# Two-layer hybrid decoder trunk: the router reads the rows before they are normed, and the norm scale moves into the experts' silu, product and softmax

## The chip, the cores and the metric

The kernel runs on one core of one Trainium2 chip. The metric is the device time of one execution in microseconds (us). TensorE is called PE here, VectorE DVE, ScalarE ACT, GpSimd POOL and the queue that issues most transfers SP.

## What is computed

The trunk has two layers over 256 tokens of width 1024. The change lies in the last part of the second layer: after the residual sum `h` is complete, the rows are normed, a router picks two of eight experts for each token, and the experts' SwiGLU outputs are added with softmax weights.

```python
def rms_norm(x, g):
    y = x * rsqrt(mean(x * x, axis=-1) + EPS)
    return y * g

def moe_swiglu(xn, w_router, we_gate, we_up, we_down):    # xn = rms_norm(h, ln_ffn1)
    logits = xn @ w_router                                # 256 x 8
    top_v, top_i = top_k(logits, 2)
    top_w = softmax(top_v)
    gates = sum(one_hot(top_i, 8) * top_w[..., None], axis=-2)
    y = 0
    for e in range(8):                                    # D_FF = 3584
        y = y + gates[:, e:e+1] * ((silu(xn @ we_gate[e]) * (xn @ we_up[e])) @ we_down[e])
    return y                                              # h + y is the output
```

The norm's scale is one number for each token. It doesn't change the order of a token's logits, and a product of a row with a matrix can be scaled after as well as before.

## The kernel before, in words

Each engine runs a program that is written out by hand in one order; semaphores tie the programs together, so an instruction that waits holds up everything behind it on its engine. Tokens lie in two blocks of 128 (`TB = 2`). Products of full precision are made of split operands: ACT writes the high part of a weight piece (`w_hi`, `split_high`, L1091), DVE the low part (`w_lo`, `split_low`, L1555), and PE does three matmuls for each (`TERMS`, L465). A piece is 128 x 1024; six pieces (`SPLIT_SLOTS`) and six chunks of two pieces (`RAW_SLOTS`) are held at a time, and SP fetches a chunk when DVE has split the one in its slot.

After the last projection of the attention part, `h` is final, and the router stage begins. PE transposes the 16 blocks of `h` (L477). ACT sums the squares of the rows (`sumsq`, L1100) and writes the turned rows' high parts (`xT_hi`, L1127), DVE computes the norm's scale by a chain of small steps (`rsqrt`, L1571 to L1577) and writes the low parts (`xT_lo`, L1597) and the normed rows `xr` (L2067). PE forms turned logits (`wr_hi`, `wr_lo`), DVE copies them, PE turns them back (L921). DVE ranks the logits of both token blocks, works out which token uses which expert (`rt`), the softmax weights through ACT's exponential (L1438), the positions (`posc`, from PE's products of masks with `before` and `ones`), the table of all units (`tab`), and marks the tokens of unit 0 in `onehot` (L2120). Then it works out tables for up to three extra units (`over`, L2127 to L2140), which are needed only if an expert has more than 128 tokens.

A unit is one expert with up to 128 of its tokens. For unit 0 PE gathers the rows by products of `xr` with `onehot` (`gather`) and turns the slots' gate and token number (`turn`, `cur`); ACT and DVE split the gathered rows (`gathered`, L1447 and L2148). A later unit's rows come by an indirect transfer from `x_rows`, which POOL has written from `xr`. A unit has seven steps over D_FF; the gate products go to one bank, ACT takes their silu (`silu_g`, L1457), the up products to another, DVE multiplies them (`act_f`, L2188), PE turns the product (L986), ACT and DVE split it (L1461, L2192), and PE multiplies by the down weights. ACT keeps a unit's gate in `gslot` (`keep_gate`, L1467). `keep_busy(n, 6)` (L485) is n transposes into a bank that nobody reads.

Of the kernel before, what the change touches and what calls it, by code (L numbers as in the profile page):

```python
# [12 lines left out]
P = 128  # L13
# [19 lines left out]
def hybrid_trunk(  # L33
# [37 lines left out]
    with ExitStack() as ctx:  # L71
# [27 lines left out]
        earlier = sb("earlier", [P, NE, NE])  # L99
        gain_rows = sb("gain_rows", [P, P])  # L100
# [9 lines left out]
        wr_hi = sb("wr_hi", [P, KD, NE], F32R)  # L110
        wr_lo = sb("wr_lo", [P, KD, NE], F32R)
# [50 lines left out]
        with part:  # L162
# [8 lines left out]
            lgT = sb("lgT", [NE, S], scope=part)  # L171
            lg = sb("lg", [P, TB, NE], scope=part)
            rt = sb("rt", [P, 16, TB, NE], scope=part)
            cmp = sb("cmp", [P, 3, TB, NE, NE], scope=part)
            posc = sb("posc", [P, TB + 1, NE], scope=part)
            tab = sb("tab", [P, UNITS, 3, TB], scope=part)
            cur = sb("cur", [P, 4, TB], scope=part)
            over = sb("over", [P, 8, NE], scope=part)
            unit_f = sb("unit_f", [1, 4], scope=part)
            unit_i = sb("unit_i", [1, 4], I32, scope=part)  # L180
            gslot = sb("gslot", [P, 1], scope=part)
            xg = sb("xg", [P, D], scope=part)
            y_out = sb("y_out", [P, D], scope=part)
            slot = sb("slot", [P, 2], scope=part)
# [208 lines left out]
        def _(pool):  # L393
# [28 lines left out]
            fill(earlier[:, :, :], 1.0, [[1, NE], [-1, NE]], -1, 0, ALU.is_ge, 0.0)  # L422
            fill(headsel[:, :, :], 0.0, [[-1, LH], [0, P]], 0, 1, ALU.not_equal, 1.0)
# [10 lines left out]
            pool.wait_ge(sem("rows_normed"), 8)  # L434
            pool.dma_start(tokens(x_rows), xr[:, :, :]).then_inc(sem("x_rows_here"), 16)
# [27 lines left out]
        def _(pe):  # L463
# [444 lines left out]
            transpose_rows(lambda t, k: h[:, t, k * P:(k + 1) * P], KD, after=("rows_added", 2 * TB))  # L908
            wr = (wr_hi, wr_lo)
            keep_busy(24, 6)  # L910
            for k in range(KD):
                if k % 2 == 0:
                    pe.wait_ge(sem("xT_ready"), 26 + k // 2 + 1)
                for a, b in TERMS:
                    last = mm(B[4][0:NE, 0:S], wr[a][:, k, :], xT[b][:, k, :],
                              k == 0 and (a, b) == (0, 0), k == KD - 1 and (a, b) == TERMS[-1])
            last.then_inc(sem("logits_psum"), 1)

            pe.wait_ge(sem("logits_copied"), 1)
            for t in range(TB):  # L920
                last = pe.transpose(B[5][:, S + t * NE:S + (t + 1) * NE], lgT[:, t * P:(t + 1) * P], ident[0:NE, 0:NE])  # L921
            last.then_inc(sem("logits_psum"), 1)

            keep_busy(10, 6)
            pe.wait_ge(sem("routed"), 1)
# [8 lines left out]
            def gather(u):  # L934

                pe.wait_ge(sem("onehot_ready"), u + 1)
                for k in range(KD):
                    for t in range(TB):
                        last = mm(B[k // 4][:, (k % 4) * P:(k % 4 + 1) * P], xr[:, t, k * P:(k + 1) * P],
                                  F(onehot[:, t, :]), t == 0, t == TB - 1)  # L940
# [73 lines left out]
            def start_unit(u):  # L1014

                gather(u)
                turn(u)
                pe.wait_ge(sem("gather_ready"), 2 * u + 2)
                e_in(C_MOE, 0, FFN_CHUNKS * u)

# [41 lines left out]
            for j in range(NU_MAX):  # L1062
                n_over = pe.value_load(unit_i[0:1, 3:4], min_val=0, max_val=NU_MAX)
                with pe.If(n_over > j):
                    start_unit(NE + j)
# [4 lines left out]
        def _(act):  # L1070
# [364 lines left out]
            norm_rows(("tile_evacuated", (copied(TILE_OUT1),) * TB))  # L1435
            high_T(KD, 26, G["ffn1"])
            act.wait_ge(sem("top_diff"), 1)
            act.activation(rt[:, 8, :, 0:1], rt[:, 7, :, 0:1], ACT.Exp).then_inc(sem("top_exp"), 1)  # L1438
            act.activation(small[:, 63:64], iota[:, 0:1], ACT.Silu)
# [11 lines left out]
            def e_silu(c, more, n):  # L1451
# [5 lines left out]
                act.activation(silu_g[:, 0:FC], B[0][:, :], ACT.Silu).then_inc(sem("esilu_done"), 1)  # L1457
# [6 lines left out]
            def keep_gate(u):  # L1464

                act.wait_ge(sem("slots_known"), u + 1)
                act.activation(gslot[:, :], slot[:, 0:1], ACT.Copy).then_inc(sem("turned"), 1)  # L1467

            def unit(u, last=False):
# [43 lines left out]
                if not last:  # L1513
                    act.wait_ge(sem("y_scaled"), 2 * u + 2)
                    keep_gate(u + 1)

            gathered(0)
            keep_gate(0)
# [4 lines left out]
            for j in range(NU_MAX):  # L1523
                n_over = act.value_load(unit_i[0:1, 3:4], min_val=0, max_val=NU_MAX)
                with act.If(n_over > j):
# [4 lines left out]
                    keep_gate(NE + j)  # L1530
# [4 lines left out]
        def _(dve):  # L1535
# [275 lines left out]
            chain(dve.tensor_copy(wr_hi[:, :, :], w_router[:, :, :]))  # L1811
            dve.tensor_tensor(wr_lo[:, :, :], w_router[:, :, :], F(wr_hi[:, :, :]), ALU.subtract).then_inc(
# [243 lines left out]
            add_tile(TILE_OUT1 + 1, C_OUT1 + 2, 1)  # L2056

# [7 lines left out]
            low_T(KD, 26, G["ffn1"])  # L2065
            for t in range(TB):
                dve.tensor_scalar(xr[:, t, :], h[:, t, :], stat[:, 4, 36 + t:37 + t], None, ALU.mult).then_inc(  # L2067
                    sem("rows_normed"), 1)
            dve.wait_ge(sem("logits_psum"), 1)
# [219 lines left out]
```

## Time and profile before

| | |
|---|---|
| median of 3 runs | 1539.64 us (1538.36 to 1540.07) |
| the profiled execution's own time | 1541.83 us |
| its span in the profile | 1540.1 us |
| PE busy | 1476.1 us, 96% of the span |
| DVE busy | 1210.4 us, 79% |
| ACT busy | 1049.4 us, 68% |
| POOL busy | 39.3 us, 3% |
| last matmul of the projection before the router starts | 528.74 us after the span's start |
| first matmul of unit 0's experts | 553.96 us |

Busy shares are means over stages with different limits. The router stage, from about 529 to 554 us, is read by itself: there PE has little of its own to do and its program holds 68 matmuls of `keep_busy`.

### The profile page before, as it was taken

What the parts mean: (1) busy time and instruction counts of PE and PEld (TensorE: products, weight loads), DVE (VectorE), ACT (ScalarE), POOL (GpSimd) and SP (SyncE); (2) the same over time, 40 slices, a digit from 0 to 9 for tenths busy, and PEclk for the clock granted to TensorE, in tenths of its full rate; (3) what the DMA queues carried; (4) which work ended last, traced back from release to release, by engine and by line L of the source; (5) the groups of instructions that cost most, each with busy time, mean ns of one, the idle gap of its engine ahead of it and who ended that gap; (6) DMA issues with size and microseconds to landing.
All of it is one profiled execution on the core that took longest, in us unless ns stands there. A gap on an engine that the chain in (4) does not pass through costs nothing.

```text
span 1540.1 us, 23433 instructions
## 1 busy us (share of the span) xinstructions
PE 1476.1 (96%) x7724; PEld 1258.2 (82%) x7724; DVE 1210.4 (79%) x1571; ACT 1049.4 (68%) x1381; POOL 39.3 (3%) x83
## 2 busy tenths in 40 slices
PE   6998999999998899999999999999999999999995
PEld 5987999999786778878878888888888888887884
DVE  6967555445566589989989989989989998998993
ACT  5664544444485457788777878878778878787872
POOL 1000000000000000000010000000000000000000
PEclk9999999999999999999999999999999999999997
DMA  7554365555251369999999999999999999999990
GB/s 256 175 178 137 103 227 184 177 184 180 70 178 55 110 230 388 375 356 378 390 348 380 390 357 375 390 370 357 393 377 343 393 380 351 390 379 355 396 391 33
DMA packets 191804, 442.05 MB, mean 287 GB/s; under 512 B 8750, under 2 KB 20364, under 8 KB 191756
## 3 DMA queue, kind: packets, MB, share of 16 engines
q1 hardware_dynamic: 188636, 429.90, 77.1%
q0 software_dynamic: 3120, 11.54, 2.7%
q8 instruction: 28, 0.46, 0.1%
q14 instruction: 20, 0.16, 0.0%
HBM read 433.54 MB, written 7.86 MB: 287 GB/s over the span
## 4 chain that ended last, share of the span: by engine, by line
PE 90%; DVE 6%; ACT 3%; issue 1%; DMA 0%; ACTq 0%; SPq 0%; DVEq 0%
PE bank L465 87%; PE bank L986 2%; DVE w_lo L1555 1%; ACT w_hi L1091 1%; DVE xT_lo L1597 1%; PE bank L477 0%; ACT xT_hi L1127 0%; DVE aT_lo L2192 0%; PE bank L485 0%; ACT aT_hi L1461 0%; DMA late<-in_mem_dram 0%; PE bank L653 0%; ACT scr L1409 0%; DVE stat L1575 0%; DVE stat L1576 0%
## 5 line engine op out<-in xcount | busy, mean ns | idle before, releaser
L1555 DVE TENSOR_TENSOR w_lo<-raw,w_hi 128x1024 fp32r<-128x1024 f32 (+1 forms) x832 | 959.3, 1196 | 202.7 <-ACT w_hi L1091 190.7
L1091 ACT ACTIVATE w_hi<-raw 128x1024 fp32r<-128x1024 f32 (+1 forms) x832 | 841.2, 1043 | 246.4 <-PE bank L465 239.6
L465 PE MATMUL bank<-w_hi,xT_hi 128*128 128x512 f32 (+4 forms) x1118 | 436.0, 390 | 11.9 <-DVE w_lo L1555 3.6
L465 PE MATMUL bank<-w_hi,xT_lo 128*128 128x512 f32 (+4 forms) x1118 | 429.0, 384 | 0.0
L465 PE MATMUL bank<-w_lo,xT_hi 128*128 128x512 f32 (+4 forms) x1118 | 428.4, 383 | 0.0
L465 PEld LDWEIGHTS bank<-w_hi,xT_hi 128*128 128x128 f32 x1118 | 211.0, 189 | 54.4 <-issue 6.6
L465 PEld LDWEIGHTS bank<-w_hi,xT_lo 128*128 128x128 f32 x1118 | 210.9, 189 | 40.3
L465 PEld LDWEIGHTS bank<-w_lo,xT_hi 128*128 128x128 f32 x1118 | 211.2, 189 | 37.2
L465 PE MATMUL bank<-w_hi,aT_hi 128*128 128x512 f32 x560 | 220.1, 393 | 7.3 <-DVE aT_lo L2192 5.7
L465 PE MATMUL bank<-w_lo,aT_hi 128*128 128x512 f32 x560 | 220.3, 393 | 0.0
L465 PE MATMUL bank<-w_hi,aT_lo 128*128 128x512 f32 x560 | 218.2, 390 | 0.0
L465 PE MATMUL bank<-xT_hi,w_hi 128*128 128x256 f32 x544 | 155.2, 285 | 2.4 <-DVE w_lo L1555 1.7
L465 PE MATMUL bank<-xT_hi,w_lo 128*128 128x256 f32 x544 | 154.7, 284 | 0.0
L465 PE MATMUL bank<-xT_lo,w_hi 128*128 128x256 f32 x544 | 154.7, 284 | 0.0
L465 PEld LDWEIGHTS bank<-w_hi,aT_hi 128*128 128x128 f32 x560 | 105.1, 188 | 33.0 <-issue 7.9
L465 PEld LDWEIGHTS bank<-w_hi,aT_lo 128*128 128x128 f32 x560 | 105.1, 188 | 23.2
L465 PEld LDWEIGHTS bank<-w_lo,aT_hi 128*128 128x128 f32 x560 | 105.3, 188 | 21.1
L465 PEld LDWEIGHTS bank<-xT_hi,w_hi 128*128 128x128 f32 x544 | 103.9, 191 | 3.4 <-DVE w_lo L1555 2.0
L465 PEld LDWEIGHTS bank<-xT_lo,w_hi 128*128 128x128 f32 x544 | 103.9, 191 | 0.2
L465 PEld LDWEIGHTS bank<-xT_hi,w_lo 128*128 128x128 f32 x544 | 103.8, 191 | 0.0
L1461 ACT ACTIVATE aT_hi<-bank 128x512 fp32r<-128x512 f32 x56 | 33.5, 598 | 52.0 <-PE bank L986 51.9
L2192 DVE TENSOR_TENSOR aT_lo<-bank,aT_hi 128x512 fp32r<-128x512 f32 x56 | 38.6, 689 | 14.4 <-ACT aT_hi L1461 10.7
(345 smaller groups left out, 790.5 us busy)
## 6 DMA issues: line engine op xcount, KB each, us to landing
raw<-in_we_gate_dram SPq DMA_DIRECT2D x112, 1024.0 KB, 7.8
raw<-in_we_up_dram SPq DMA_DIRECT2D x112, 1024.0 KB, 8.0
raw<-in_we_down_dram SPq DMA_DIRECT2D x112, 1024.0 KB, 7.2
raw<-in_w_gate_dram SPq DMA_DIRECT2D x14, 1024.0 KB, 5.1
raw<-in_w_up_dram SPq DMA_DIRECT2D x14, 1024.0 KB, 5.1
raw<-in_w_down_dram SPq DMA_DIRECT2D x14, 1024.0 KB, 4.8
raw<-in_w_in_dram SPq DMA_DIRECT2D x16, 768.0 KB, 4.9
raw<-in_w_out_dram SPq DMA_DIRECT2D x8, 1024.0 KB, 5.0
```

Source lines behind the costliest of these rows:

```text
L465: return pe.matmul(o, a, b, start=start, stop=stop, skip_group_check=True, **kw)
L986: last = pe.transpose(B[2][:, q * P:(q + 1) * P], act_f[:, q * P:(q + 1) * P], ident[:, :])
L1091: act.activation(split_piece(w_hi, c, shape, half), raw_piece(c, shape, half), ACT.Copy).then_inc(hi_ready, 1)
L1461: act.activation(aT_hi[:, :, 0:P], B[2][:, :].rearrange("p (q s) -> p q s", q=FB), ACT.Copy).then_inc(sem("eaT_hi"), 1)
L1555: dve.tensor_tensor(split_piece(w_lo, c, shape, half), raw_piece(c, shape, half), F(split_piece(w_hi, c, shape, half)), ALU.subtract).then ...
L1597: ins = dve.scalar_tensor_tensor(out=xT_lo[:, k0 + k, :], in0=B[bank0 + b][:, kk * S:(kk + 1) * S], scalar=1.0 if gain is None else gains[ ...
L2192: dve.tensor_tensor(aT_lo[:, :, 0:P], B[2][:, :].rearrange("p (q s) -> p q s", q=FB), F(aT_hi[:, :, 0:P]), ALU.subtract).then_inc(sem("eaT ...
```

## The change

- PE transposes `h` into four banks; ACT and DVE copy them as plain fp32 into `act_f` and `silu_g`, which are free then. The router's logits are fp32 matmuls of these with `wr_gain`, the router weights times the norm's weights, which DVE has made long before. They come out with tokens in partitions, unscaled by the norm.
- DVE ranks each token block when its logits are there (`route`), and marks unit 0's tokens in `onehot` directly from `posc`. The chain for the norm's scale, the logits' difference and the exponential come after that.
- Unit 0 is gathered from `h` itself; `x_rows` is written from `h`; ACT copies `h` to `xr` for extra units. So the expert products lack the norm's scale: `turn` brings it along in `cur` (three columns in place of two), `gslot` holds gate and scale, silu takes `scale=gslot[:, 1:2]`, the product becomes a `scalar_tensor_tensor` with the scale, and the difference of logits is multiplied by it before the exponential.
- `gate_weights` (softmax weights and unit table) stands behind `gathered(0)` on DVE, `turn(0)` behind the first gate product on PE, `keep_gate(u)` ahead of the first silu of each unit on ACT, and `extra_units` between units 6 and 7 on DVE.
- `keep_busy` has 20 and 6 matmuls in place of 24, 10, 12 and 22.

```diff
@@ pool
-            pool.wait_ge(sem("rows_normed"), 8)
-            pool.dma_start(tokens(x_rows), xr[:, :, :]).then_inc(sem("x_rows_here"), 16)
+            pool.wait_ge(sem("rows_added"), 3 * TB)
+            pool.dma_start(tokens(x_rows), h[:, :, :]).then_inc(sem("x_rows_here"), 16)
@@ tensor
-            transpose_rows(lambda t, k: h[:, t, k * P:(k + 1) * P], KD, after=("rows_added", 2 * TB))
-            keep_busy(24, 6)
...
-            keep_busy(10, 6)
-            pe.wait_ge(sem("routed"), 1)
+            hT = (act_f, silu_g)
+            for t in range(TB):
+                pe.wait_ge(sem("rows_added"), 2 * TB + t + 1)
+                for k in range(KD):
+                    last = pe.transpose(B[2 * t + k // 4][:, (k % 4) * P:(k % 4 + 1) * P], h[:, t, k * P:(k + 1) * P], ident[:, :])
+                    if k % 4 == 3:
+                        last.then_inc(sem("router_psum"), 1)
+            for t in range(TB):
+                pe.wait_ge(sem("router_first"), t + 1)
+                pe.wait_ge(sem("router_second"), t + 1)
+                for k in range(KD):
+                    last = mm(B[4 + t][:, 0:NE], hT[t][:, k * P:(k + 1) * P], wr_gain[:, k, :], k == 0, k == KD - 1)
+                last.then_inc(sem("logits_psum"), 1)
+
+            keep_busy(20, 6)
+            pe.wait_ge(sem("routed"), TB)
...
             def turn(u):
+                pe.wait_ge(sem("cur_ready"), u + 1)
                 for t in range(TB):
-                    last = mm(B[3][:, S:S + 2], F(onehot[:, t, :]), cur[:, 2:4, t], t == 0, t == TB - 1)
+                    last = mm(B[3][:, S:S + 3], F(onehot[:, t, :]), cur[:, 2:5, t], t == 0, t == TB - 1)
...
-            keep_busy(12, 6)
-            gather(0)
-            turn(0)
-            keep_busy(22, 6)
-            pe.wait_ge(sem("gather_ready"), 2)
-            e_in(C_MOE, 0, 0)
+            keep_busy(6, 6)
+            start_unit(0, first=True)
@@ scalar
+            act.wait_ge(sem("tile_evacuated"), copied(TILE_OUT1))
+            for t in range(TB):
+                sumsq(h[:, t, 0:512], 2 * t, xr[:, t, 0:512]).then_inc(sem("sumsq_ready"), 1)
+            for t in range(TB):
+                act.wait_ge(sem("router_psum"), 2 * t + 1)
+                act.activation((act_f, silu_g)[t][:, 0:512], B[2 * t][:, :], ACT.Copy).then_inc(sem("router_first"), 1)
...
-                act.activation(silu_g[:, 0:FC], B[0][:, :], ACT.Silu).then_inc(sem("esilu_done"), 1)
+                act.activation(silu_g[:, 0:FC], B[0][:, :], ACT.Silu, scale=gslot[:, 1:2]).then_inc(sem("esilu_done"), 1)
...
                 for j in (4, 5):
                     split_high(p0 + j, UP, more, lap)
+                keep_gate(u)
+                act.wait_ge(sem("turned"), u + 1)
                 e_silu(C_MOE + 2, more, None)
@@ vector
+            for t in range(TB):
+                dve.wait_ge(sem("router_psum"), 2 * t + 2)
+                dve.tensor_copy((act_f, silu_g)[t][:, 512:1024], B[2 * t + 1][:, :]).then_inc(sem("router_second"), 1)
+            def route(t):
+                dve.wait_ge(sem("logits_psum"), t + 1)
+                chain(dve.tensor_copy(lg[:, t, :], B[4 + t][:, 0:NE]))
...
+                step(dve.tensor_tensor(equal, other, own, ALU.is_equal))
+                step(dve.tensor_tensor(above, other, own, ALU.is_gt))
+                settle()
+                chain(dve.tensor_tensor(equal, equal, earlier[:, :, :], ALU.mult))
+                chain(dve.tensor_reduce(rt[:, 0, t, :], cmp[:, t], AX, ALU.add))
+                dve.tensor_scalar(rt[:, 5, t, :], rt[:, 0, t, :], 1.5, None, ALU.is_lt).then_inc(sem("routed"), 1)
...
-                dve.tensor_tensor(act_f[:, 0:FC], B[1][:, :], silu_g[:, 0:FC], ALU.mult).then_inc(sem("eact_done"), 1)
+                dve.scalar_tensor_tensor(out=act_f[:, 0:FC], in0=B[1][:, :], scalar=gslot[:, 1:2], in1=silu_g[:, 0:FC],
+                                         op0=ALU.mult, op1=ALU.mult).then_inc(sem("eact_done"), 1)
...
             gathered(0)
+            gate_weights()
+            split_low(2 * C_MOE + 4, UP)
             slots(0)
-            for j in (4, 5):
-                split_low(2 * C_MOE + j, UP)
+            split_low(2 * C_MOE + 5, UP)
             with dve.Fori(0, NE - 1) as u:
                 unit(u)
+            extra_units()
             unit(NE - 1, last=True)
```

`gate_weights` and `extra_units` hold what stood in DVE's program ahead of `gathered(0)`: the first the softmax weights, `tab` and `cur`, the second the tables of the extra units, now for all three at once (18 instructions).

PE's program between the logits and the first expert product, before (`before` and `ones` are constant masks, `ident` alone is `keep_busy`, `onehot,xr` the gather, `cur,onehot` the turn, and the last row is the first expert matmul):

```order
L921 MATMUL bank<-ident,lgT 128x8 [waits logits_copied]
L921 MATMUL bank<-ident,lgT 128x8
L485 MATMUL bank<-ident 128x128 x10
L465 MATMUL bank<-rt,before 128x8 [waits routed]
L465 MATMUL bank<-rt,ones 128x8
L465 MATMUL bank<-rt,before 128x8
L465 MATMUL bank<-rt,ones 128x8 x2
L485 MATMUL bank<-ident 128x128 x12
L465 MATMUL bank<-onehot,xr 128x128 [waits onehot_ready]
L465 MATMUL bank<-cur,onehot 128x2 x2
L485 MATMUL bank<-ident 128x128 x22
L465 MATMUL bank<-w_hi,xT_hi 128x512 [waits lo_ready,gather_ready]
```

The same place after the change:

```order
L468 MATMUL bank<-wr_gain,silu_g 128x8 x7
L488 MATMUL bank<-ident 128x128 x20
L468 MATMUL bank<-rt,before 128x8 [waits routed]
L468 MATMUL bank<-rt,ones 128x8
L468 MATMUL bank<-rt,before 128x8
L468 MATMUL bank<-rt,ones 128x8 x2
L488 MATMUL bank<-ident 128x128 x6
L468 MATMUL bank<-onehot,h 128x128 [waits onehot_ready]
L468 MATMUL bank<-onehot,h 128x128 x15
L468 MATMUL bank<-w_hi,xT_hi 128x512 [waits lo_ready,gather_ready]
...
L468 MATMUL bank<-cur,onehot 128x3 [waits cur_ready]
L468 MATMUL bank<-cur,onehot 128x3
```

The 22 transposes between gather and first product are gone, and the turn has moved behind the 24 matmuls that begin with the row on `gather_ready`.

DVE's program from the end of the gathered rows' low parts into unit 0, before (the first row is the last wait of `gathered(0)`, then `slots(0)` and pieces 4 and 5):

```order
L2148 SCALAR_TENSOR_TENSOR xT_lo<-bank,gains,xT_hi 128x128 [waits gather_hi]
L2148 SCALAR_TENSOR_TENSOR xT_lo<-bank,gains,xT_hi 128x128 x3
L2157 COPY slot<-bank 128x2 [waits turn_psum]
L2160 TENSOR_SCALAR no_token<-slot,row_no 128x1 [waits slot_copied]
L2163 SCALAR_TENSOR_TENSOR rows_next<-slot,no_token 128x1 [waits no_token_ready]
L1555 TENSOR_TENSOR w_lo<-raw,w_hi 128x1024 [waits hi_ready] x2
```

And after the change:

```order
L2169 SCALAR_TENSOR_TENSOR xT_lo<-bank,gains,xT_hi 128x128 [waits gather_hi]
L2169 SCALAR_TENSOR_TENSOR xT_lo<-bank,gains,xT_hi 128x128 x3
L2115 TENSOR_SCALAR rt<-rt 128x2 [waits top_exp]
...
L2126 COPY tab<-rt 128x2x8 x2
L2132 COPY cur<-tab 128x6 [waits dve_step]
L1563 TENSOR_TENSOR w_lo<-raw,w_hi 128x1024 [waits hi_ready]
L2178 COPY slot<-bank 128x3 [waits turn_psum]
L2181 TENSOR_SCALAR no_token<-slot,row_no 128x1 [waits slot_copied]
L2184 SCALAR_TENSOR_TENSOR rows_next<-slot,no_token 128x1 [waits no_token_ready]
L1563 TENSOR_TENSOR w_lo<-raw,w_hi 128x1024 [waits hi_ready]
```

The gate's chain now stands behind the gathered rows, and piece 5 waits on DVE behind the turn.

## Rows read from the trace of the kernel before

**Rows 1.** The page's chain that ended last, by engine.

```profile
PE 90%; DVE 6%; ACT 3%; issue 1%; DMA 0%; ACTq 0%; SPq 0%; DVEq 0%
```

**Rows 2.** Who PE waited for from 554 to 1540 us: total, times, longest.

```profile
PE bank L465 <- DVE aT_lo L2192: 5.7, 8, 1.4
PE bank L465 <- DVE w_lo L1555: 1.4, 8, 0.2
```

**Rows 3.** Timeline of DVE, router stage: start, us, instruction, idle time and its releaser.

```profile
529.17 0.69 DVE L1834 TENSOR_TENSOR h<-bank,h 128x512 f32<-128x512 f32 x1 [2.03 <-PE bank L465]
530.65 0.16 DVE L2061 TENSOR_REDUCE stat<-stat 128x2 f32<-128x4 f32 x1 [0.79 <-ACT xr L1100]
...
533.66 3.23 DVE L1597 SCALAR_TENSOR_TENSOR xT_lo<-bank,gains,xT_hi 128x256 fp32r<-128x256 f32 x8 [0.28 <-ACT xT_hi L1127]
...
538.91 0.36 DVE L2073 TENSOR_SCALAR lg<-bank,stat 128x8 f32<-128x8 f32 x2 [0.38 <-PE bank L921]
...
544.34 0.17 DVE L2117 COPY cur<-tab 128x6 f32<-128x6 f32 x1
544.55 0.60 DVE L2120 TENSOR_SCALAR onehot<-iota,cur 128x128 fp32r<-128x128 f32 x2
...
551.77 2.14 DVE L2148 SCALAR_TENSOR_TENSOR xT_lo<-bank,gains,xT_hi 128x128 fp32r<-128x128 f32 x8
553.84 0.14 DVE L2157 COPY slot<-bank 128x2 f32<-128x2 f32 x1
```

**Rows 4.** Timeline of PE in the same stage.

```profile
528.97 2.04 PE L477 MATMUL bank<-ident,h 128*128 128x128 f32 x16
...
541.69 0.39 PE L465 MATMUL bank<-rt,before 128*128 128x8 f32 x2 [1.58 <-DVE rt L2093]
...
543.10 2.80 PE L485 MATMUL bank<-ident 128*128 128x128 f32 x12
545.69 3.88 PE L465 MATMUL bank<-onehot,xr 128*128 128x128 f32 x32
549.40 0.51 PE L465 MATMUL bank<-cur,onehot 128*128 128x2 f32 x4
549.77 2.60 PE L485 MATMUL bank<-ident 128*128 128x128 f32 x22
553.96 0.50 PE L465 MATMUL bank<-w_hi,xT_hi 128*128 128x512 f32 x1 [1.60 <-DVE xT_lo L2148]
```

**Rows 5.** Timeline of ACT, gather and start of unit 0.

```profile
549.60 1.14 ACT L1447 ACTIVATE xT_hi<-bank,gains 128x128 fp32r<-128x128 f32 x4 [0.64 <-PE bank L465]
...
559.77 0.60 ACT L1457 ACTIVATE silu_g<-bank 128x512 f32<-128x512 f32 x1 [3.05 <-PE bank L465]
```

**Rows 6.** Groups of the whole span by form: busy us, mean ns.

```profile
L1461 ACT ACTIVATE aT_hi<-bank 128x512 fp32r<-128x512 f32 x56 | 33.5, 598 | 52.0 <-PE bank L986 51.9
L1511 ACT ACTIVATE y_out<-bank,gslot 128x512 f32<-128x512 f32 x14 | 8.9, 685 | 6.4 <-PE bank L465 6.4
L2188 DVE TENSOR_TENSOR act_f<-bank,silu_g 128x512 f32<-128x512 f32 x56 | 38.5, 688 | 0.0
L2171 DVE SCALAR_TENSOR_TENSOR ys_lo<-bank,gslot,ys_hi 128x512 fp32r<-128x512 f32 x2 | 1.4, 747 | 6.7 <-ACT ys_hi L1511 6.7
```

**Rows 7.** Windows: busy time (x count) of PE, PEld, DVE, ACT, POOL; PE clock; DMA.

```profile
540.00:541.00 1.00, 0.11 (x2) 0.00 (x0) 0.91 (x4) 0.00 (x0) 1.00 (x2) 1.00 1.03 414
543.00:544.00 1.00, 1.00 (x7) 1.00 (x7) 0.93 (x8) 0.71 (x2) 0.00 (x0) 0.50 1.02 393
553.00:554.00 1.00, 0.04 (x1) 0.04 (x1) 0.97 (x5) 0.00 (x0) 0.00 (x0) 1.00 0.00 0
620.00:640.00 20.00, 20.00 (x94) 16.55 (x93) 18.32 (x17) 15.62 (x18) 0.00 (x0) 1.00 1.03 383
```

**Rows 8.** Timeline at the start of unit 7.

```profile
1406.73 4.63 DVE L1555 TENSOR_TENSOR w_lo<-raw,w_hi 128x1024 fp32r<-128x1024 f32 x4 [1.91 <-ACT w_hi L1091]
1408.01 0.50 PE L465 MATMUL bank<-w_hi,xT_hi 128*128 128x512 f32 x1 [0.18 <-DVE w_lo L1555]
```

More of the change, by code:

```diff
@@ L422, in _ @@
             fill(earlier[:, :, :], 1.0, [[1, NE], [-1, NE]], -1, 0, ALU.is_ge, 0.0)
+            for j in range(NU_MAX):
+                step(pool.memset(nth[:, j, :], float(j + 1)))
             fill(headsel[:, :, :], 0.0, [[-1, LH], [0, P]], 0, 1, ALU.not_equal, 1.0)
@@ L1466, in keep_gate @@
                 act.wait_ge(sem("slots_known"), u + 1)
-                act.activation(gslot[:, :], slot[:, 0:1], ACT.Copy).then_inc(sem("turned"), 1)
+                act.activation(gslot[:, :], slot[:, 0:2], ACT.Copy).then_inc(sem("turned"), 1)
             def unit(u, last=False):
@@ L1514, in unit @@
                     act.wait_ge(sem("y_scaled"), 2 * u + 2)
-                    keep_gate(u + 1)
             gathered(0)
-            keep_gate(0)
+            act.wait_ge(sem("top_diff"), 1)
+            act.activation(rt[:, 8, :, 0:1], rt[:, 7, :, 0:1], ACT.Exp).then_inc(sem("top_exp"), 1)
+            act.activation(small[:, 63:64], iota[:, 0:1], ACT.Silu)
             with act.Fori(0, NE - 1) as u:
@@ L2075, in _ @@
-            settle()
-            for t in range(TB):
-                own = lg[:, t, :].unsqueeze(2).to_broadcast([P, NE, NE])
-                other = lg[:, t, :].unsqueeze(1).to_broadcast([P, NE, NE])
-                step(dve.tensor_tensor(cmp[:, 0, t], other, own, ALU.is_gt))
-                step(dve.tensor_tensor(cmp[:, 1, t], other, own, ALU.is_equal))
-            settle()
-            for t in range(TB):
-                step(dve.tensor_tensor(cmp[:, 1, t], cmp[:, 1, t], earlier[:, :, :], ALU.mult))
@@ L2101, in _ @@
-            chain(dve.tensor_tensor(rt[:, 10, :, 0:1], rt[:, 8, :, 0:1], rt[:, 9, :, 0:1], ALU.mult))
-            for t in range(TB):
-                step(dve.tensor_scalar(rt[:, 11, t, :], rt[:, 1, t, :], rt[:, 9, t, 0:1], None, ALU.mult))
-            settle()
-            for t in range(TB):
-                step(dve.scalar_tensor_tensor(out=rt[:, 12, t, :], in0=rt[:, 2, t, :], scalar=rt[:, 10, t, 0:1],
-                                              in1=rt[:, 11, t, :], op0=ALU.mult, op1=ALU.add))
@@ L2108, in _ @@
-            dve.wait_ge(sem("slots_psum"), 1)
-            chain(dve.tensor_copy(posc[:, :, :].rearrange("p t e -> p (t e)"), B[5][:, 0:3 * NE]))
-            for n, src in enumerate((posc[:, 0:TB, :], rt[:, 5], rt[:, 12])):
-                step(dve.tensor_copy(tab[:, 0:NE, n, :].rearrange("p e t -> p t e"), src))
-            chain(dve.tensor_copy(cur[:, 3, :], row_no[:, 0:TB]))
+            scale = stat[:, 4, 36:36 + TB]
+            step(dve.tensor_copy(cur[:, 3, :], scale))
+            step(dve.tensor_copy(cur[:, 4, :], row_no[:, 0:TB]))
@@ new lines, in _, with gate_weights @@
+            chain(dve.tensor_tensor(rt[:, 6], rt[:, 4], rt[:, 3], ALU.subtract))
+            chain(dve.tensor_reduce(rt[:, 7, :, 1], rt[:, 6], AX, ALU.add))
+            dve.tensor_tensor(rt[:, 7, :, 0], rt[:, 7, :, 1], scale, ALU.mult).then_inc(sem("top_diff"), 1)
+            def gate_weights():
+                dve.wait_ge(sem("top_exp"), 1)
+                chain(dve.tensor_scalar(rt[:, 9, :, 0:1], rt[:, 8, :, 0:1], 1.0, None, ALU.add))
+                chain(dve.reciprocal(rt[:, 9, :, 0:1], rt[:, 9, :, 0:1]))
+                chain(dve.tensor_tensor(rt[:, 10, :, 0:1], rt[:, 8, :, 0:1], rt[:, 9, :, 0:1], ALU.mult))
+                for t in range(TB):
+                    step(dve.tensor_scalar(rt[:, 11, t, :], rt[:, 1, t, :], rt[:, 9, t, 0:1], None, ALU.mult))
+                settle()
+                for t in range(TB):
+                    step(dve.scalar_tensor_tensor(out=rt[:, 12, t, :], in0=rt[:, 2, t, :], scalar=rt[:, 10, t, 0:1],
+                                                  in1=rt[:, 11, t, :], op0=ALU.mult, op1=ALU.add))
+                settle()
+                for n, src in enumerate((posc[:, 0:TB, :], rt[:, 5], rt[:, 12])):
+                    step(dve.tensor_copy(tab[:, 0:NE, n, :].rearrange("p e t -> p t e"), src))
+                settle()
+                current(0)
```

135 lines of the change are left out of this document (61 added, 74 removed).

## The prediction

> **What bounds the kernel now.** I read the page's chain that ended last first: 90% of the span is PE's own work [rows 1]. Then the waits of PE in the expert stage, 554 to 1540 us: the longest sum is 5.7 us, once per unit for the last product's low part, and 1.4 us are eight waits of 0.2 us for a weight piece at a unit's start [rows 2]. So that stage is as long as its matmuls, and nothing in it gets shorter. What is left is the stage between, and the timelines show it: PE transposes `h` from 528.97 and begins the first expert matmul at 553.96 [rows 4], 25.0 us later. Its last wait there is for DVE, whose timeline has nearly no gap [rows 3]: the norm's chain 530.65 to 533.4, the turned rows' low parts to 536.9, `xr`, ranking from 538.91, softmax and tables, `onehot` ready at 545.15, then 6.6 us of tables for extra units, and only at 551.77 the gathered rows' low parts, though ACT had their second half ready at 550.74 [rows 5]. The change takes most of these off DVE's path.
>
> **The router up to the marks.** The 16 transposes end at 531.0 as before; the first eight at about 530.0. DVE copies half of block 0 out of its bank: no such row here is shown, the nearest is the sum of the same size out of a bank, 0.69 us [rows 3]. So logits of block 0 can start at 530.8, when PE's own transposes are through. They are 8 fp32 matmuls with 8 columns. Masks of the same shape took 1.41 us for 5 (541.69 to 543.10), 0.28 each, partly at the lower clock; the gather 3.88 us for 16, 0.24 [rows 4]. I take 0.23: block 0 to 532.7, block 1 to 534.5; by 0.28 it would be 0.8 us more. Ranking both blocks took 2.7 us (538.91 to PE's masks at 541.69); now block 0's lies under PE's logits of block 1, and half, 1.4 us, is left: 535.95. PE meanwhile has 20 transposes of `keep_busy`. 22 took 2.60 us, the last one's latency included, so 0.11 each and 2.2 us for 20, to 536.7: PE comes 0.7 us after the masks are ready to go. Masks 1.4 us (538.1), copy of `posc` 0.2, marks 0.60 [rows 3]: `onehot` is ready at about 538.9 against 545.15.
>
> **Gather and first product.** The gather takes 3.9 us as before, to 542.7. ACT needs 1.14 us for the second half [rows 5], 543.85, DVE half of 2.14 us [rows 3], 544.95, and the first expert matmul starts at 545.05 in place of 553.96: **8.9 us gained**. DVE must do the norm's chain in this time: 2.75 us (530.65 to 533.4) and some 1.1 us for `cur`, difference and product, so 538.9 to 542.75. It comes to the first half of the gathered rows 0.7 us after ACT, is through at 543.8, and so just in time for the second. Here the cover is about 0.05 us; every further delay of that chain counts in full. The exponential, the table load and the gate's chain lie behind, under the 5.8 us of the first product (553.96 to 559.77 [rows 4, 5]).
>
> **Start of unit 0.** The turn is now between the first product and the up product: 0.5 us on PE [rows 4]. Piece 5's low part waits on DVE behind the slots, which wait for the turn: turn done at 551.35, three small instructions to 551.9 (0.14 us for the first [rows 3], with its latencies about 0.2 each), piece 5 at 1.16 us (4.63 for 4 [rows 8]) to 553.1, while PE is through with piece 4 at 552.65: 0.45 us of waiting. ACT copies `gslot` and takes the silu, both behind the slots, 0.8 us, then piece 6 at about 1.05 and DVE's 1.16: 555.0, where PE wants it at 554.45: 0.6 us. Before, there was a wait of 0.2 [rows 2] and no turn. **Loss 1.35 us.** The SP fetches that piece 5 frees also come this much nearer to PE, but six chunks are held.
>
> **Steady stage.** Silu gets a scale from memory. The same read out of a bank took 598 ns without and 685 with such a scale [rows 6]: 0.09 us. DVE's product goes from 688 to about the 747 of the same form with a scalar from memory [rows 6]: 0.06 us, 56 times. DVE is busy 18.32 of 20 us in a window of this stage [rows 7], so 1.4 us of each step of 16.9 are free and this is hidden; without that cover it would be 3.4 us. The silu is hidden too, but for unit starts, where piece 6 stands behind it and PE waits 0.18 us for that piece [rows 8]: 6 times 0.09, **loss 0.5 us**. The Trainium skill, page ScalarE: Activation LUTs, section What ACT_TABLE_LOAD costs, gives about 93 ns for each pointer operand of an ACTIVATE; the rows give 87, and the loss would come to 0.56 us by the page. The extra units' tables now stand at one unit's start. They are 18 small instructions, partly overlapped; before, such steps came every 0.2 us, and I take 2.7 us. DVE is idle 1.91 us there [rows 8], so **0.8 us are lost**, between nothing and 1.7 (0.2 us each without overlap). `keep_gate` moves from one idle place of ACT to another: nothing. Three memsets of POOL at the start and one small instruction less on DVE: nothing, under the first transfers and under PE's work.
>
> **Sum without the clock:** 8.9 - 1.35 - 0.5 - 0.8 = 6.25 us.
>
> **The clock.** In the window 543 to 544 the granted clock is 0.50, that is 1.2 GHz [rows 7], and 12 transposes took 2.80 us there, where 22 took 2.60 at 2.4 GHz [rows 4]. Ahead of it lay 1.58 us of idle PE and masks of 8 columns. Another idle time of 1.60 us, before 553.96, was followed by nothing of the kind: 1.00 [rows 7]. The changed program has more of what came before the fall: 3.7 us of matmuls with 8 columns, and an idle PE of about 2.3 us (542.7 to 545.05) with no transposes in it, where 22 lay before. The low stretch of before lasted some 3 us and cost little, since DVE was late anyway. Now PE's work stands on the path nearly everywhere, and such a stretch costs half its length, 1.6 us. [...] I count one such stretch: gain 4.65 us. The profiled execution took 1541.83 us and would take 1537.2; the median of the runs lies 2.2 us lower, and the forecast for it is 1539.64 - 4.65 = **1535.0 us**.
>
> **The rivals.**
> - *No fall of the clock* (chance 0.28): 1533.4 us. For it: the gap at 553 was not followed by one.
> - *Forecast, one stretch at 1.2 GHz* (0.41): 1535.0; its own range is 1534 to 1536.5.
> - *Two or three stretches, or a router priced at the upper bounds* (0.22): if transposes run at 1.2 GHz ahead of the masks, 20 of them take 4.6 us and the marks come 2.4 us later, and the first product loses another 1.6 us: gain about 2, 1537.6; with 0.8 us more for the logits 1538.4. This is within 0.2% of before.
> - *Slower: PE at 1.2 GHz for the whole stage* (0.06). Logits, transposes, masks, gather, turn and first product are some 17 us of PE's work at 2.4 GHz; all of it at half speed adds over 12 us and gives about 1546. It decides from 9.3 us of loss on (6.25 plus 3.1). Against it: the fall in before gave way again under transposes and gather, at 549.77 transposes came every 0.11 us [rows 4].
> - *DVE becomes the bound of the steady stage* (0.03): the product would have to take 1.4 us more, not 0.06, before the first is felt, and 1.55 more to end 0.2% slower; the row of 747 ns speaks against it. A transfer as the bound belongs here: the DMA share is 1.03 in 620 to 640 [rows 7]. If the weights set the pace, the gain would be that of the next fetch, which hangs on piece 5's low part: near 5 us, and the losses at unit starts would vanish. That too lands at 1535.
>
> **Range and chances.** The low end is the case without a fall, with the extra tables hidden and a little cheaper logits: 1532.4. The high end is the case of three stretches: 1538.9. A measurement of this kernel tells about 0.2%, 3.1 us, from no change. Faster than 1536.6: no fall, most of one stretch: 0.70. Within: 0.23. Slower: 0.07.
>
> **What would show it.** In the profile of the changed kernel: `onehot` marks end near 539 and the first expert matmul is near 545, 16 us after the transposes' start; PE's wait ahead of it is for DVE's `xT_lo`; the logits' matmuls lie 0.23 us apart; PE waits about 0.5 us each for pieces 5 and 6 of unit 0; unit 7 begins with a wait near 1 us for `w_lo`; silu is at 0.68, the product at 0.75, and no other wait is new between units. The expert stage is 1.5 to 3 us longer from its first matmul to its end. The prediction is wrong if the clock stays low for long, if DVE's chain for the norm's scale ends late and pushes the gathered rows, or if the product or silu bring new waits in each of the 56 steps.

## The result, and the profile after

The changed kernel takes 1546.07 us (median of 14 runs, 1541.73 to 1548.45), the kernel before 1540.96 beside it (1538.36 to 1543.04): ratio 1.0031, 95% interval 1.0023 to 1.0039. It is slower by 5.1 us, where 4.65 us of gain were forecast. The profiled execution took 1544.55 us, with a span of 1542.8.

Yet the router stage went nearly as the prediction said. PE's timeline in the profile after, with the rows that answer to [rows 4]:

```profile
531.09 2.04 PE L915 MATMUL bank<-ident,h 128*128 128x128 f32 x16
533.00 1.92 PE L468 MATMUL bank<-wr_gain,act_f 128*128 128x8 f32 x16
534.78 1.93 PE L468 MATMUL bank<-wr_gain,silu_g 128*128 128x8 f32 x16
536.57 4.05 PE L488 MATMUL bank<-ident 128*128 128x128 f32 x20
540.45 0.29 PE L468 MATMUL bank<-rt,before 128*128 128x8 f32 x2
...
541.48 0.85 PE L488 MATMUL bank<-ident 128*128 128x128 f32 x6
542.64 3.84 PE L468 MATMUL bank<-onehot,h 128*128 128x128 f32 x32 [0.30 <-DVE onehot L2092]
548.87 0.50 PE L468 MATMUL bank<-w_hi,xT_hi 128*128 128x512 f32 x1 [2.39 <-DVE xT_lo L2169]
...
554.49 0.51 PE L468 MATMUL bank<-cur,onehot 128*128 128x3 f32 x4
...
556.83 0.50 PE L468 MATMUL bank<-w_hi,xT_hi 128*128 128x512 f32 x1 [0.35 <-DVE w_lo L1563]
...
558.93 0.50 PE L468 MATMUL bank<-w_hi,xT_hi 128*128 128x512 f32 x1 [0.44 <-DVE w_lo L1563]
```

From the transposes of `h` to the first expert matmul it is 17.78 us, where it was 24.99: 7.2 us less. The 20 transposes of `keep_busy` took 4.05 us. The windows say why (busy time of PE, PEld, DVE, ACT, POOL, then PE's clock and the DMA share):

```profile
537.00:540.00 3.00, 3.00 (x16) 3.00 (x15) 1.15 (x7) 0.00 (x0) 0.00 (x0) 0.50 1.01 388
545.00:546.00 1.00, 1.00 (x12) 1.00 (x11) 0.83 (x7) 0.87 (x4) 0.00 (x0) 1.00 0.00 0
```

They ran at 1.2 GHz, half the clock, and DVE, done with ranking at 538.25, then sat idle for the masks:

```profile
538.08 0.17 DVE L2086 TENSOR_SCALAR rt<-rt 128x16 f32<-128x16 f32 x1
541.76 0.18 DVE L2090 COPY posc<-bank 128x24 f32<-128x24 f32 x1 [3.51 <-PE bank L468]
...
546.07 1.12 DVE L2169 SCALAR_TENSOR_TENSOR xT_lo<-bank,gains,xT_hi 128x128 fp32r<-128x128 f32 x4
547.69 1.13 DVE L2169 SCALAR_TENSOR_TENSOR xT_lo<-bank,gains,xT_hi 128x128 fp32r<-128x128 f32 x4 [0.50 <-ACT xT_hi L1453]
```

The time was lost elsewhere. The transposes of `h` begin 2.1 us later than in [rows 4], though little of the code ahead of them is changed. And in the expert stage the sums of PE's waits grew by less than was forecast. From 545 us on, total, times and longest:

```profile
PE bank L468 <- DVE aT_lo L2214: 5.8, 8, 1.4
PE bank L468 <- DVE w_lo L1563: 3.1, 9, 0.7
PE bank L468 <- DVE xT_lo L2169: 2.4, 1, 2.4
```

That is 1.7 us more for `w_lo` than in [rows 2], where 2.15 had been forecast (0.85 in unit 0, 0.5, and 0.8 at unit 7). But from the turn of `act_f` in unit 0's first step to that of the last step of unit 7 it is 947.3 us, after 941.4: 5.9 more. A middle step shows no wait in either kernel and takes 16.96 us in place of 16.87, every time. Both turns of one such step and the first, second and last of its 24 down products, before:

```profile
950.52 0.60 PE L986 MATMUL bank<-ident,act_f 128*128 128x128 f32 x4
...
956.45 0.39 PE L465 MATMUL bank<-w_hi,aT_hi 128*128 128x512 f32 x1
956.68 0.39 PE L465 MATMUL bank<-w_lo,aT_hi 128*128 128x512 f32 x1
...
961.72 0.39 PE L465 MATMUL bank<-w_hi,aT_lo 128*128 128x512 f32 x1
...
967.39 0.27 PE L986 MATMUL bank<-ident,act_f 128*128 128x128 f32 x1
```

And after:

```profile
949.14 0.60 PE L988 MATMUL bank<-ident,act_f 128*128 128x128 f32 x4
...
955.05 0.39 PE L468 MATMUL bank<-w_hi,aT_hi 128*128 128x512 f32 x1
955.29 0.39 PE L468 MATMUL bank<-w_lo,aT_hi 128*128 128x512 f32 x1
...
960.42 0.40 PE L468 MATMUL bank<-w_hi,aT_lo 128*128 128x512 f32 x1
...
966.10 0.27 PE L988 MATMUL bank<-ident,act_f 128*128 128x128 f32 x1
```

The 23 distances between 24 down products are 5.27 us before and 5.37 after: 229 and 233.5 ns each. The other 48 products of a step, with `xT`, lie some 227 ns apart in both. (Over all products from 600 to 1500 us the means are 229.1 and 233.1 ns with `aT`, 227.7 and 227.5 with `xT`.) The clock was 1.00 in both stretches. So the same matmuls on operands of the same shape take longer, and only those that read `aT`.

`aT` is the stationary operand of these matmuls: PE loads a 128x128 piece of it ahead of each one (PEld), and the 512 columns that then stream past are those of the weights, `w_hi` or `w_lo`. The loads' own time is the same, only the idle time between them grew. One of the three groups of loads, 600 to 1500 us (count, busy, mean ns, idle before), in the kernel before and after:

```profile
L465 PEld LDWEIGHTS bank<-w_lo,aT_hi 128*128 128x128 f32 x416 | 78.2, 188 | 15.5
L468 PEld LDWEIGHTS bank<-w_lo,aT_hi 128*128 128x128 f32 x416 | 78.1, 188 | 18.7
```

Over the three groups the idle time is 56.6 us before and 61.7 after.

What differs is where `aT` lies. The change removes `wr_hi` and `wr_lo` (256 bytes of each partition apiece), adds `wr_gain` (256) and `nth` (96), and all that is declared behind them moves down by 160 bytes: `aT_hi` from byte 165184 to 165024, `aT_lo`, 4096 further, likewise. `w_hi`, `w_lo`, `xT_hi` and `xT_lo` stand ahead of them and didn't move; all four begin 128 bytes beyond a multiple of 1024. The four pieces of `aT_hi` that a step loads lie 1024 bytes apart, so all have the remainder by 1024 of the first.

### The profile page after: what moved, and what is told of

The parts are those of the page before. It is cut to its first block, busy times and chain, and to the rows that moved or that the text cites. A ratio compares the mean times of both kernels' runs of the same rounds, so it can differ in the third digit from the quotient of the medians.

```text
span 1542.8 us, 23338 instructions
## 1 busy us (share of the span) xinstructions
PE 1478.9 (96%) x7688; PEld 1255.2 (81%) x7688; DVE 1204.6 (78%) x1547; ACT 1053.2 (68%) x1377; POOL 42.8 (3%) x86
## 4 chain that ended last, share of the span: by engine, by line
PE 90%; DVE 5%; ACT 3%; issue 1%; DMA 0%; ACTq 0%; SPq 0%; DVEq 0%
PE bank L468 87%; PE bank L988 2%; DVE w_lo L1563 1%; ACT w_hi L1090 1%; DVE xT_lo L1605 0%; PE bank L480 0%; DVE aT_lo L2214 0%; PE bank L488 0%; ACT aT_hi L1467 0%; DMA late<-in_mem_dram 0%; PE bank L656 0%; ACT scr L1408 0%; ACT xT_hi L1126 0%; DVE stat L1583 0%; DVE stat L1582 0%
## 5 line engine op out<-in xcount | busy, mean ns | idle before, releaser
L468 PE MATMUL bank<-w_hi,aT_lo 128*128 128x512 f32 x560 | 221.4, 395 | 0.0
```

Of the source, the lines that this page charges most:

```text
L468: return pe.matmul(o, a, b, start=start, stop=stop, skip_group_check=True, **kw)
```

## The experiments

Each run stands beside runs of the kernel before on the same chip; the kernel before had medians of 1540.3 to 1541.4 in all of them. "Ratio" is the time over that of the kernel before, with its 95% interval; "step" is the distance in us between the turns of `act_f` in the middle steps of units 1 to 6.

**Theories.** L: the address of `aT` sets the distance of the down products, and costs what the expert stage lost. Rivals: the new forms of silu and product slow the step; the clock takes it; the router gains nothing.

### First four: shifts, and the old forms

`a_aligned` is the changed kernel with eight fp32 ahead of `cos`, which brings `aT_hi` to 165056, a multiple of 64. `b_shifted` is the kernel before with the same line (165216), `b_shift_behind` the kernel before with it behind `aT_lo`, so that `silu_g` and all behind move and `aT` doesn't.

```diff
+        pad32 = sb("pad32", [P, 8])
         cos = sb("cos", [P, TB, HALF])
```

> The changed kernel with one unused tile of 32 bytes ahead of cos, so that aT_hi and aT_lo begin at a multiple of 64 bytes again, as in the kernel before; nothing else differs. Theory A (the place of aT in SBUF makes the down products' 24 matmuls of a step some 4 ns slower each): a middle step of a unit goes from 16.96 back to 16.87 us, the expert stage gets 5 to 6 us shorter and layer 0's SwiGLU about 1 us, so 1539.5 us, that is 6 to 7 us under the changed kernel and 1 to 2 under the one before, and the clock decides the rest. Theory B (silu with a scale from memory and the three-operand product slow PE's work): the step stays at 16.96 and the time at 1546.

> The kernel before with the same unused 32 bytes ahead of cos, which shifts aT_hi and aT_lo from a multiple of 64 bytes to 32 beyond one. Theory A: a middle step goes from 16.87 to 16.96 us and the time up by 6 to 7 us, to 1547. Theory B: no change.

> The kernel before with the unused 32 bytes between aT_lo and silu_g: aT stays where it was, and all that is declared behind it in this part (silu_g, act_f, onehot and the router's tiles) is shifted. Theory A, aT alone: no change, step 16.87. Rival A2 (the place of silu_g and act_f, which ACT and DVE write while PE multiplies, is what counts): step 16.96 and 6 us more.

`a_old_forms` is the changed kernel with the experts' silu and product in their forms of before; it leaves the norm's scale out of the experts.

```diff
-act.activation(silu_g[:, 0:FC], B[0][:, :], ACT.Silu, scale=gslot[:, 1:2])
+act.activation(silu_g[:, 0:FC], B[0][:, :], ACT.Silu)
-dve.scalar_tensor_tensor(out=act_f[:, 0:FC], in0=B[1][:, :], scalar=gslot[:, 1:2], in1=silu_g[:, 0:FC],
-                         op0=ALU.mult, op1=ALU.mult)
+dve.tensor_tensor(act_f[:, 0:FC], B[1][:, :], silu_g[:, 0:FC], ALU.mult)
```

> The changed kernel with the silu without its scale and the product as a plain two-operand product; it leaves the norm's scale out of the experts. The layout is that of the changed kernel. Theory A: step 16.96, time within 1 us of the changed kernel, since silu is on the path only at a unit's start (0.5 us). Theory B: step 16.87 and about 6 us less than the changed kernel.

| | median us | ratio, 95% | step |
|---|---|---|---|
| a_aligned | 1547.52 | 1.0032, 1.0021 to 1.0043 | 16.97 |
| b_shifted | 1547.10 | 1.0040, 1.0028 to 1.0052 | 16.95 |
| b_shift_behind | 1540.98 | 0.9994, 0.9985 to 1.0002 | 16.85 |
| a_old_forms | 1542.12 | 1.0006, 0.9998 to 1.0015 | 16.96 |

A shift of 32 bytes alone makes the kernel before 6 us slower; a shift behind `aT` does nothing. So the layout costs, and `silu_g`, `act_f` and the rest of the experts' tiles aren't what counts. My reading of it as "a multiple of 64 or not" fell: at 165056 nothing got better. The old forms leave the step at 16.96, so the forms aren't its cause. Their median is 4 us below the changed kernel's 1546.07, which is from another lot of runs; of this the way from the first to the last turn of `act_f` (946.9 us in place of 947.3) explains 0.4.

### The next four: `aT` put where it was

`a_same` is the changed kernel again, as the base. `a_at_before` puts `aT_hi` back to 165184, `a_at_128` puts it 128 bytes beyond a multiple of 1024 (166016), as `xT` stands. Only `aT` and what is declared behind it move.

```diff
+            ahead = sb("ahead", [P, 40], scope=part)
             aT_hi = sb("aT_hi", [P, FB, S], F32R, scope=part)
```

`a_at_128` has 248 in place of 40. `a_busy8` has `keep_busy(8, 6)` in place of `keep_busy(20, 6)`.

> The changed kernel itself again, in one call with the next three. Its times spread from 1541.7 to 1548.5 us and those with a mean granted clock of 0.989 are some 4 us shorter than those of 0.984. Theory C (besides slower steps, low stretches of the clock from the router's logits to the first product cost up to 3 us more in some runs): median near 1546, step 16.96, and the profile shows a low stretch that begins between the transposes of h and the first product. Rival C2 (the spread comes from the stages ahead of the router alone): the low stretches in the router stage are the same in every profile.

> The changed kernel with 160 unused bytes directly ahead of aT_hi, so that it begins at byte 165184 of a partition as before (after the change: 165024; in the first try at alignment: 165056, and steps stayed slow). Theory A3 (the place of aT counts, but finer than by a multiple of 64): step 16.85 to 16.87 and 5.5 to 6.5 us less than the changed kernel in this call. Rival A4 (some other tile between cos and aT_lo, such as stat or small, makes the difference, since they stay shifted here): step 16.96, no gain.

> The changed kernel with 992 unused bytes directly ahead of aT_hi, so that it begins at byte 166016, which is 128 beyond a multiple of 1024, as raw, w_hi, w_lo, xT_hi and xT_lo are, whose matmuls lie 227 ns apart. If the place relative to the weights' tiles counts: the down products' spacing goes from 233.5 to 227, below the 229 of the kernel before, the step to 16.80 and the time 8 to 9 us under the changed kernel. If only the place of before is good: no gain over 16.96.

> The changed kernel with 8 transposes in place of 20 between the logits and the masks. In the profile after, the 20 took 4.05 us at the lower clock and the masks began 2.3 us after DVE had routed. Theory: the masks follow the routing at once, the first expert matmul comes 1 to 2.4 us earlier relative to the transposes of h; but PE is idler and the clock may fall again, in the gather or the first product, at up to 1.7 us. So between 2.4 us less and 1 more; 1 us less expected. Steps stay at 16.96.

| | median us | ratio, 95% | step |
|---|---|---|---|
| a_same | 1545.22 | 1.0022, 1.0013 to 1.0032 | 16.96 |
| a_at_before | 1535.34 | 0.9965, 0.9951 to 0.9978 | 16.87 |
| a_at_128 | 1532.38 | 0.9945, 0.9931 to 0.9958 | 16.80 |
| a_busy8 | 1541.46 | 1.0002, 0.9993 to 1.0011 | 16.96 |

This decides that the place of `aT` costs the step. With `aT` where the kernel before had it, the changed kernel is 6.0 us faster than that kernel (1541.35 in these runs), and 0.3 us from the forecast of 1535.0. That it is so near is in part luck: the forecast took 4.65 us off a base of 1539.64, the median of three runs. In its PE timeline the waits are the same as in the changed kernel, so what went away in the expert stage is the longer distance of the matmuls:

```profile
533.38 3.73 PE L489 MATMUL bank<-ident 128*128 128x128 f32 x20
...
539.45 3.84 PE L469 MATMUL bank<-onehot,h 128*128 128x128 f32 x32 [0.30 <-DVE onehot L2093]
545.68 0.50 PE L469 MATMUL bank<-w_hi,xT_hi 128*128 128x512 f32 x1 [2.39 <-DVE xT_lo L2170]
551.27 0.50 PE L469 MATMUL bank<-cur,onehot 128*128 128x3 f32 x4
553.60 0.50 PE L469 MATMUL bank<-w_hi,xT_hi 128*128 128x512 f32 x1 [0.36 <-DVE w_lo L1564]
```

At 166016 the down products of `a_at_128` lie 226.5 ns apart (5.21 us for 23), about as all others:

```profile
948.52 0.39 PE L469 MATMUL bank<-w_hi,aT_hi 128*128 128x512 f32 x1
948.74 0.39 PE L469 MATMUL bank<-w_lo,aT_hi 128*128 128x512 f32 x1
...
953.73 0.39 PE L469 MATMUL bank<-w_hi,aT_lo 128*128 128x512 f32 x1
```

`a_busy8` came out of its expected span: 3.8 us below the changed kernel, where at most 2.4 had been expected. Its trace doesn't show why, since from the transposes of `h` to the first expert matmul it takes 17.60 us in place of 17.76.

### Is it the layout alone, and does it hold for the kernel before?

`b_at_128` and `b_at_160` are the kernel before with `ahead` at 208 and 216 fp32: `aT_hi` at 166016 and at 166048. The second has the remainder by 1024 that the changed kernel has, 160. `a_128_busy8` and `a_128_forms` put the two other edits on `a_at_128`; the second again leaves out the norm's scale in the experts.

> The kernel before with 832 unused bytes ahead of aT_hi alone, which puts the turned product aT where the changed kernel at its best layout had it (byte 166016 of a partition instead of 165184). Theory L (the address of aT sets the spacing of the down products, and the change's own gain adds to it): the step falls from 16.87 to 16.80 us, so the time is 56 steps times 0.07, some 4 us, below the kernel before, about 1537, and the changed kernel at this address (1532.4) still leads it by about 5, the router's gain. Rival (the gain at this address came with the changed router, not with the layout): the step stays at 16.87 and the time within 1 us of the kernel before.

> The kernel before with 864 unused bytes ahead of aT_hi alone: aT at byte 166048, 32 bytes further than in the run above and with the same remainder by 1024 (160) as in the changed kernel (165024). Theory L, with aT alone as the cause: down products at 233 to 235 ns, the step 16.95 to 16.97 us, the time 5 to 7 us above the kernel before, 1546 to 1548. Rival (another tile that the earlier shifted kernel moved with aT, among them the tables and the attention's tiles, is the cause): spacing 227 to 229 ns, step 16.80 to 16.87, the time at or below the kernel before.

> The changed kernel at its best layout (aT at 166016), with 8 instead of 20 of the throwaway transposes ahead of the turns of xT_lo. If the 3.8 us that this edit gave at the other layout come from the router stage and the clock behind it, they come again: 1529 to 1530. If they were a difference between two lots of runs, the time stays at 1532 to 1533.

> The changed kernel at its best layout, with the experts' silu and product in their forms of before (no scale from a table; the norm's scale is left out of the experts). By the unit starts read so far (0.07 to 0.08 us each, and under 1 us at unit 7) the forms are worth 0.6 to 1.5 us: 1531 to 1532. If the 3 to 4 us that the same edit gave at the other layout belong to it, 1528 to 1529.

| | median us | ratio, 95% | step |
|---|---|---|---|
| b_at_128 | 1538.62 | 0.9984, 0.9975 to 0.9993 | 16.80 |
| b_at_160 | 1547.59 | 1.0045, 1.0032 to 1.0059 | 16.96 |
| a_128_busy8 | 1533.57 | 0.9950, 0.9936 to 0.9964 | 16.80 |
| a_128_forms | 1532.48 | 0.9949, 0.9935 to 0.9963 | 16.80 |

In the kernel before too, 32 bytes between 166016 and 166048 are worth 9.0 us: the layout acts without the change. But `b_at_128` is only 1.7 us below the 1540.29 of the kernel before beside it, where 4 had been expected. Its trace has the gain of the steps (938.3 us from the first to the last turn of `act_f`, after 941.4, and 0.7 us in the first layer's SwiGLU). Its 11 executions fall into two groups, 3 of 1534.4 to 1535.5 us with a mean granted clock of 0.986 to 0.987 and 8 of 1538 to 1541 with 0.983 to 0.984. So it is the clock that took back part of the gain in most of them; why is open.

At 166016 the changed kernel leads the kernel before by 6.2 us, at 165184 by 6.0: what the change does by itself, without the layout. The first of these compares two lots of runs; by each one's distance from the kernel before beside it, it is 7.3. The profiles, read from the first transpose of `h` to the end of the span, give 5.3 us at 166016 (1007.9 and 1002.5) and 5.4 at 165184 (1011.1 and 1005.7). Neither fewer throwaway transposes nor the old forms show a gain at the good layout (ratios of 0.9950 and 0.9949 beside 0.9945, each known to some 0.0014, which is 2 us); the further gains that I had held possible didn't come.

### What is left: 3 us

`a_at_160` is the changed kernel with `ahead` at 256 fp32 (166048), `a_same2` and `a_forms2` repeat two kernels.

> The changed kernel with 1024 unused bytes ahead of aT_hi alone: aT at byte 166048 instead of 165024, the same remainder (160) by 1024. If that remainder is what counts, all is as in the changed kernel: step 16.96 us, 1545 to 1546. If the changed kernel's last 3 to 4 us (which neither the step nor the unit starts explain) belong to something else that the 1024 bytes move, 1541 to 1542.

> The changed kernel once more, beside the old forms once more. 1545 to 1546 again. Its profile shows whether the half-clock stretches ahead of the router stage (near 21, 62, 83 and 141 us in both its profiles so far; first product with aT at 220.5) belong to this program, or change from one execution to the next.

> The old forms of silu and product in the experts at the changed kernel's own layout once more (the norm's scale is left out of the experts). At the better layout they were worth nothing (1532.48 beside 1532.38). If the 3 to 4 us of their first run were chance between lots of runs, 1544 to 1545 now, with half-clock stretches as in the changed kernel; if they belong to this program, 1542 again, with the stretches near 60 and 135 us and the first product with aT at 218.4.

| | median us | ratio, 95% | step |
|---|---|---|---|
| a_at_160 | 1546.20 | 1.0036, 1.0023 to 1.0049 | 16.96 |
| a_same2 | 1544.88 | 1.0025, 1.0016 to 1.0034 | 16.96 |
| a_forms2 | 1542.83 | 1.0013, 1.0004 to 1.0022 | 16.96 |

1024 bytes further on, nothing changes. That fits the remainder as what counts, but proves it only weakly, since the remainders 192 and 352 gave the same slow step. The profiles of `a_same` and `a_same2`, one and the same program, have spans of 1545.2 and 1541.5. Four stretches of the first at half the clock, of 3.4 us each, are missing in the second: near 82, 140, 550 and 1526 us. Windows of `a_same` on the first three:

```profile
82.00:85.00 3.00, 2.60 (x8) 2.63 (x9) 2.96 (x9) 1.77 (x3) 0.00 (x0) 0.53 1.01 372
140.00:143.00 3.00, 2.69 (x15) 2.32 (x13) 2.70 (x5) 1.65 (x7) 0.00 (x0) 0.54 0.03 8
550.00:553.00 3.00, 3.00 (x9) 2.32 (x8) 1.67 (x6) 1.10 (x2) 0.00 (x0) 0.50 0.00 0
```

And of `a_same2`:

```profile
82.00:85.00 3.00, 2.53 (x15) 2.56 (x16) 2.96 (x9) 1.95 (x5) 0.00 (x0) 1.00 1.06 373
140.00:143.00 3.00, 1.99 (x10) 1.61 (x10) 3.00 (x10) 3.00 (x9) 0.00 (x0) 1.00 0.46 127
550.00:553.00 3.00, 3.00 (x15) 2.49 (x14) 0.44 (x1) 0.00 (x0) 0.00 (x0) 1.00 0.00 0
```

The two executions differ where the stretches are. The transposes of `h` begin 1.3 us later in `a_same`, the way from the first expert matmul to the first turn of `act_f` is 1.6 us longer, and the last part, after the last turn, 0.8; the rest is equal. So 3.7 us between two executions of one program are such stretches, 1.3 of them ahead of the change's own code. But the old forms came out 4 and 2 us below the changed kernel in the two lots, which pure chance doesn't explain well. Why they, and the fewer transposes, do so at this layout and not at 166016 stays open.

## Why the prediction was wrong

**The step that failed** is "So that stage is as long as its matmuls, and nothing in it gets shorter". The first half is right; what I drew from it is that the stage could only change by waits, and the time of its matmuls stands in the sum at nothing. The distance of the matmuls grew, by some 4 ns for 24 of each 72. From its first matmul to its end the stage took 993.9 us after 986.2, 7.7 more, where 1.5 to 3 had been forecast. I had counted the removed and added tiles nowhere, though the program has them. In the two profiles this is 0.09 us in each of the 55 steps between the first and the last turn, 5.0 us, and 1.3 us more in the first layer's SwiGLU, whose products with `aT` run from 218.25 to 411.96 us before (193.7 us) and from 220.56 to 415.56 after (195.0). That is 6.3 us. By medians, putting `aT` back to its old address gains 9.9 us (1545.22 to 1535.34), nearly all of the 11.1 us by which the forecast missed. Of the 3.6 us between 9.9 and 6.3, the profiles show only stretches at half the clock (ahead of 600 us 37.5 us of them in `a_same`, 27.3 in `a_at_before`). Over all executions of the two kernels the mean granted clocks, 0.985 and 0.986, are worth only about 1 us (an estimate: the clock's share that is missing, times the span). So some 2 to 3 us have no cause shown; whether the address has a part in them is open.

**Router up to the marks.** Right in mechanism. A block's eight logits products took 1.78 us (533.00 to 534.78), 0.22 each in place of 0.23, the ranking behind the logits 1.5 us against 1.4. What came late were the masks behind the 20 transposes, by some 1.7 us (3.88 us from the first transpose to the masks against 2.2), by the half clock, which had been counted as one stretch without a place. With it the forecast of the interval, 16.1 + 1.6 = 17.7 us, met 17.78.

**Gather and first product.** PE waited 2.39 us where 2.3 was forecast. DVE's norm chain, for which only 0.05 us of cover had been counted, had more: DVE waited 0.50 us for ACT's second half.

**Start of unit 0.** Forecast 0.5 + 0.45 + 0.6 less 0.2; measured 0.51 + 0.35 + 0.44 less 0.2: 1.1 us of loss against 1.35. The whole way from the first expert matmul to the first turn of `act_f` is 18.37 us after 17.01, which is 1.36.

**Steady stage.** Silu and product, groups by form from 600 to 1500 us, count, busy, mean ns:

```profile
L2209 DVE SCALAR_TENSOR_TENSOR act_f<-bank,gslot,silu_g 128x512 f32<-128x512 f32 x52 | 38.7, 744 | 0.0
L1463 ACT ACTIVATE silu_g<-bank,gslot 128x512 f32<-128x512 f32 x52 | 35.5, 683 | 10.9 <-PE bank L468 10.9
```

683 and 744 ns met 685 and 747 [rows 6]. Both are hidden in the steps, as said: `a_128_forms` has the same step of 16.80. At equal layout (`a_at_128` and `b_at_128`) the way from the last turn of `act_f` in one unit to the first in the next is 24.55 against 24.49 us up to unit 6, 0.06 for each in place of 0.09.

**Unit 7.** DVE and PE at its start, after:

```profile
1405.85 0.17 DVE L2145 TENSOR_SCALAR over<-posc 128x8 f32<-128x8 f32 x1
...
1408.46 4.61 DVE L1563 TENSOR_TENSOR w_lo<-raw,w_hi 128x1024 fp32r<-128x1024 f32 x4
1409.72 0.50 PE L468 MATMUL bank<-w_hi,xT_hi 128*128 128x512 f32 x1 [0.68 <-DVE w_lo L1563]
```

The tables take 2.6 us against 2.7, PE waits 0.68 in place of 0.18 [rows 8]: 0.5 us of loss, not 0.8. At equal layout the whole way from unit 0's first to unit 7's last turn is 0.8 us longer than before (939.1 against 938.3), where 1.3 were forecast.

**The clock.** One stretch in the router stage, as counted, in six of the twelve profiles with the changed code; the other six have more, most of all `a_aligned`, where 10.2 us at half the clock bring the way from the transposes of `h` to the first expert matmul to 20.48 us. The idle 2.4 us ahead of the first product were followed by a granted clock of 0.50 in three of the twelve (`a_same`, the window 550 to 553 above, `a_at_160` and `a_old_forms`), and not in nine; where it fell, the way to the first turn of `act_f` was 1.6 us longer. The Trainium skill, page TensorE: Matmul & The Clock Gate, section HAM oscillation, tells of waits between bursts of matmuls after which the clock is down and the next burst starts slow. The waits of its example are longer than this one, and it doesn't settle what this one does; here it was one fall in four.

**Chances.** No rival named the layout. "Slower" had 0.07, for the clock and for DVE as the bound, and the range missed by 7 us. The rival with PE at 1.2 GHz for the whole stage gives about 1546, which is the measured time by luck: in the profile after the clock fell for 3.4 us there.

## What to carry to other kernels

Where PE is the bound, a change that adds, removes or resizes a tile ahead of a matmul's operands can change their speed: compare the distance between matmul starts in a steady step before and after, not only the waits. Test a pad ahead of operands that are read thousands of times: here 992 unused bytes were worth 13 us, twice what the change itself gave. Before a design is judged by its time, run it at the layout of the version that it is compared with; the version to keep is `a_at_128`, at 1532.38 us 0.55% below the kernel before.

## What the hardware did that was not expected

- Products with 512 columns whose stationary operand (a 128x128 piece of `aT`) begins 128 bytes beyond a multiple of 1024 started 227 ns apart; 320 beyond, 229; 160, 192 and 352 beyond, some 233 (steps of 16.80, 16.85 to 16.87 and 16.95 to 16.97 us). The loads of that operand lasted 187 to 188 ns each at all five. No rule behind these remainders was found; whether it is the address by itself or its distance from that of the weights was not tried.
- The number of stretches at half the clock differs from one execution of a program to the next; four more of them cost 3.7 us.
